# Reordering one convolution and one exponential across four engines, moving two small loads, and turning TensorE's unrolled head groups into a loop

## The reference

```python
qkv = silu(causal_depthwise_conv(qkv, conv_w))            # 4 taps along the tokens
q, k = l2_normalize(q), l2_normalize(k)                   # 16 heads of 128; v: 32 heads of 128
beta = sigmoid(beta_logit)
g = -exp(a_log) * softplus(decay_logit + dt_bias)
g = cumsum(g) inside a chunk
decay = exp(where(incl, g[:, None] - g[None, :], -inf))
a_mat = where(strict, (k * beta) @ k.T * decay, 0)
sol = triangular_solve(a_mat + I, [v * beta, k * beta * exp(g)])
attn = where(incl, q @ k.T * decay, 0)
# then, chunk after chunk: v_new = u - w @ S; o = q_dec @ S + attn @ v_new; S = S * gl + k_dec.T @ v_new
o = rmsnorm(o) * norm_w * silu(z); y_dn = o @ w_dn_out
```

## Time and profile before

| | before |
|---|---|
| median of 3 runs | 2833.82 us |
| lowest and highest | 2833.7, 2834.3 us |
| the profiled execution, its own time | 2834.3 us |
| its span, first to last instruction | 2832.6 us |
| mean granted TensorE clock | 0.996 |
| PE busy | 2775.6 us, 98% |
| PEld busy | 2072.8 us, 73% |
| DVE busy | 1252.3 us, 44% |
| ACT busy | 446.0 us, 16% |
| POOL busy | 63.7 us, 2% |
| DMA | 654.12 MB, mean 231 GB/s |

### The profile page before, as it was taken

How to read it: one execution, slowest core, us unless ns; L and a number is a source line. 1 busy time by engine, 2 the same in 40 slices (tenths; PEclk the granted TensorE clock), 3 DMA queues, 4 the chain that set the end, 5 groups by cost and what they waited for, 6 DMA issues and landing times.

```text
span 2832.6 us, 53479 instructions
## 1 busy us (share of the span) xinstructions
PE 2775.6 (98%) x22343; PEld 2072.8 (73%) x22343; DVE 1252.3 (44%) x2593; ACT 446.0 (16%) x773; POOL 63.7 (2%) x115
## 2 busy tenths in 40 slices
PE   8999999999999999999999999999999999999997
PEld 8899898898898888888899999843444444444442
DVE  6566565665664327777665652221111211112114
ACT  3121121221221111110010000131112111112110
POOL 1000000000000000000000000000000000000000
PEclk9999999999999999999999999999999999999999
DMA  7233242343344523444477556378999999999997
GB/s 218 88 122 120 90 149 91 107 142 98 102 149 107 163 90 123 130 136 137 145 210 228 178 161 226 149 293 362 422 422 422 422 422 422 422 422 422 422 422 280
DMA packets 328854, 654.12 MB, mean 231 GB/s; under 512 B 45232, under 2 KB 274736, under 8 KB 279536
## 3 DMA queue, kind: packets, MB, share of 16 engines
q1 hardware_dynamic: 328688, 651.61, 62.7%
HBM read 649.49 MB, written 2.10 MB: 230 GB/s over the span
## 4 chain that ended last, share of the span: by engine, by line
PE 88%; DMA 7%; DVE 2%; DVEq 2%; issue 1%; ACT 0%; SPq 0%; ACTq 0%
PE bank L723 14%; PE bank L675 14%; PE bank L1054 10%; PE bank L1244 9%; PE bank L975 8%; PE bank L1282 7%; DMA arena<-in_w_up_dram 7%; PE bank L1223 4%; PE bank L1109 4%; PE bank L1322 4%; PE bank L800 1%; PE bank L818 1%; PE bank L938 1%; PE bank L811 1%; PE bank L1254 1%
## 5 line engine op out<-in xcount | busy, mean ns | idle before, releaser
L675 PE MATMUL bank<-arena 128*128 128x256 f32 x2048 | 484.8, 386 | 0.0
L1244 PE MATMUL bank<-arena 128*64 128x512 f32 x2048 | 445.5, 594 | 12.3 <-DMA arena<-in_w_up_dram 12.3
L675 PEld LDWEIGHTS bank<-arena 128*128 128x128 f32 x2048 | 374.9, 190 | 52.3
L723 PEld LDWEIGHTS bank<-arena 128*128 128x128 f32 x3584 | 403.9, 192 | 4.2 <-issue 3.8
L723 PE MATMUL bank<-arena 128*128 128x128 f32 x3584 | 405.5, 275 | 0.0
L1244 PEld LDWEIGHTS bank<-arena 128*64 128x64 f32 x2048 | 144.5, 137 | 311.3 <-issue 281.5
L1054 PEld LDWEIGHTS bank<-arena 128*128 128x128 f32 x2576 | 287.8, 192 | 0.1
L1054 PE MATMUL bank<-arena 128*128 128x128 f32 x2576 | 287.8, 275 | 0.0
L975 PE MATMUL bank<-arena 128*128 128x256 f32 x1024 | 223.5, 380 | 0.0
L2356 DVE TENSOR_SCALAR arena<-bank 128x512 f32<-128x512 f32 x16 | 11.1, 691 | 465.8 <-PE bank L1244 465.8
L975 PEld LDWEIGHTS bank<-arena 128*128 128x128 f32 x1024 | 194.0, 190 | 26.7
(11 more groups left out here) (341 smaller groups left out, 2412.8 us busy)
## 6 DMA issues: line engine op xcount, KB each, us to landing
arena<-in_w_in_dram SPq DMA_DIRECT2D x72, 2048.0 KB, 8.7
arena<-in_w_up_dram SPq DMA_DIRECT2D x64, 2048.0 KB, 16.5
arena<-in_w_gate_dram SPq DMA_DIRECT2D x64, 2048.0 KB, 13.9
arena<-in_w_down_dram SPq DMA_DIRECT2D x64, 2048.0 KB, 21.1
arena<-in_w_dn_out_dram SPq DMA_DIRECT2D x16, 2048.0 KB, 8.2
arena<-in_w_glu_b_dram SPq DMA_DIRECT2D x8, 2048.0 KB, 8.2
arena<-in_w_glu_a_dram SPq DMA_DIRECT2D x8, 2048.0 KB, 8.2
arena<-in_w_mix_out_dram SPq DMA_DIRECT2D x8, 2048.0 KB, 14.3
```

The source lines that it names most:

```text
L675: last = mm(ps[bank][:, ct * T:ct * T + T], ring[:, buf, k, ct * P:ct * P + P], rhs[:, k, :], start=k == 0, stop=k == KD - 1)
L723: last = mm(regions[:, 4 * bank + place % 4], left(k), right(k), start=k == 0, stop=k == KD // 2 - 1)
L1244: last = mm(ps[bank][CAP * o:CAP * o + CAP, :], xg[:, 4 * q + k, CAP * o:CAP * o + CAP], w[:, o, k], start=False, stop=q == 3 and k == 3, ...
```

## The change

It has four parts. In the prologue, SP issues dt_bias and a_log behind the three ring slots and no longer ahead of wbd. On DVE, `conv(3)` comes ahead of `decay(1)`; on ACT, `silu(3)` comes ahead of the two exponentials of c = 1. POOL no longer waits for `conv_ready` ahead of the product of c = 1. On PE, groups 0 to 6 become a hardware loop, with the group's number in a register.

```diff
@@ SP
-            sp.dma_start(dtrow, dt_bias.partition_broadcast(P)).then_inc(bias_loaded, 16)
-            sp.dma_start(arow, a_log.partition_broadcast(P)).then_inc(bias_loaded, 16)
             sp.dma_start(wbd, in_rows(w_in[:, OFF_BD:OFF_BD + 2 * H_V])).then_inc(wbd_loaded, 16)
             for r in range(3):
                 sp.dma_start(ring[:, r], in_rows(w_in[:, group_col(r, 0):group_col(r, 0) + SC])).then_inc(slot_loaded[r], 16)
+            sp.dma_start(dtrow, dt_bias.partition_broadcast(P)).then_inc(bias_loaded, 16)
+            sp.dma_start(arow, a_log.partition_broadcast(P)).then_inc(bias_loaded, 16)
             sp.dma_start(cw[:, :, :], conv_w.rearrange("(j p) t -> p j t", p=P)).then_inc(pro_loaded, 16)
@@ POOL
                 for c in range(2):
                     pool.wait_ge(dexp_ready, 2 * gi + c + 1)
-                    if c == 1:
-                        pool.wait_ge(conv_ready, 4 * gi + 4)
                     g.tensor_tensor(Dm[:, c], Dc[:, c], upper.unsqueeze(1).to_broadcast([P, GV, P]), ALU.mult)
@@ PE
-            for g in range(GROUPS - 1):
+            with pe.Fori(0, GROUPS - 1) as g:
                 group(g, True)
                 front(g + 1)
             group(GROUPS - 1, False)
@@ ACT
                 A(Dc[:, 0], Dc[:, 0], ACT.Exp)
                 act.drain()
                 act.sem_inc(dexp_ready, 1)
+                silu(3)
+
                 act.wait_ge(arg_ready, 2 * g + 2)
                 A(Eg, ps[5][:, :].rearrange("p (a t) -> p a t", a=GV), ACT.Exp)
                 A(Dc[:, 1], Dc[:, 1], ACT.Exp)
                 act.drain()
                 act.sem_inc(dexp_ready, 1)
-                silu(3)
@@ DVE
                 decay(0)
                 join_heads(3)
+                conv(3)
                 decay(1)
-                conv(3)
```

## The result

The changed kernel takes 2869.55 us (median of 4 runs, 2868.8 to 2869.89), the kernel before on the same chip 2834.03 (4 runs, 2833.7 to 2834.3). The ratio is 1.0126, 95% interval 1.0109 to 1.0142: 35.5 us slower. The forecast was 2848.5, with 2862 as its upper end: the direction was right, and the loss is two and a half times the 14.2 us forecast.

The account below looks back on a forecast made before the run. The prediction took PE as the bound, a microsecond's delay in a group moving the end by one. It summed 2834.3 + 8.6 (reorder) + 1.2 (loads) + 4.2 (back edges) = 2848.3, said 2848.5, range 2838 to 2862.

Parts of the forecast that it names:

- The reorder, 8.6 us: DVE, ACT and POOL in the head groups: chunk 1's At comes later, PE waits at L800; 7.3 + 1.3 us.
- The chain: Join, conv(3), Silu, table load, Exps, POOL, At of chunk 1: 1.04 us later a group, 1.34 in the last.
- the row at 192.91: ACT timeline before the change: Silu's table load issued at once, 3 us ahead of its activation.
- the serial rival: ACT's table load starts only after its argument has come: reorder 14 us, total 2854; chance 0.07.
- the earlier Silu buys nothing: Transposes L776: silu(3) done at 195.16 instead of 196.51, but PE is busy until 197.58 either way; gain 0.
- POOL's removed wait is free: POOL's product of c = 1: decay(1) now follows conv(3), so the Exp wait implies the removed one; cost 0.
- The back edge, 4.2 us: PE's loop: each of six back edges asks for code not fetched ahead, 0.7 us each; ends 0 and 20.
- the L951 row: PE's one idle time with no releaser inside a run of matmuls without a wait, 1.44 us; price for edges.
- Register waits at 0: PE's loop: waits numbered from registers cost 0, worked out under queued matmuls; ends 0 and 15 us.
- The moved loads, 1.2 us: Prologue: biases land at about 29.0, DVE waits 3.1 us at L1726, PE waits 1.2 us; bounds 0 and 2.5.
- The two waits that it has: Prologue: PE waits on DVE's sums for slot 1, 0.7 us, and for slot 2, 0.5 us.
- the dear edge: PE's loop: 2 to 3.4 us at each of six back edges, 12 to 20 us, total 2860; chance 0.15.

Follow-up runs that it names:

- e5: Kernel before with only POOL's wait on conv_ready removed, DVE and ACT in their old order: 2870.21 us, 1.0133.
- e7: Kernel before with the reorder, plus two z0 fill products moved between the first products of the two chunks at solve level 0: 2832.94 us, 0.9999.
- e13: Whole changed kernel, plus two z0 fill products moved between the first products of the two chunks at solve level 0: 2856.22 us, 1.0084 to the kernel before.
- e8: Kernel before with the reorder, and a copy in place of the Silu of slot 3: 2836.54 us, 1.0011.
- e3: Kernel before with only dt_bias and a_log issued behind the ring loads: 2837.09 us, 1.0017.
- e12: The changed kernel measured again on another chip: 2871.10 us, 1.0133 to the kernel before.

## Why the prediction was right in kind and short in size

**The reorder, 8.6 us: right.** The waits at L798 grew by 7.9 us. The chain held link by link: 0.97 a group against 1.04, and 1.36 of wait in the last group against 1.34. The table load was issued ahead of its argument, as taken from the row at 192.91; the serial rival is refuted. The Trainium skill (ScalarE: Activation LUTs, What ACT_TABLE_LOAD costs) makes its 2.66 us for a switch of a load of 1.28 and a drain of 1.38. The trace agrees on the load, 1.28, and shows no drain: the next activation starts 0.01 us behind the load. That the earlier Silu buys nothing, and that POOL's removed wait is free, held as well, the latter only because the new order takes its place (e5).

**The back edge, 4.2 us: the first wrong step, a mis-sized term.** "I take 0.7 for each, half of the L951 row, 4.2 us in all" measured 9.7 in the loop alone and 13.2 with the rest of the change. The mechanism was as told: the body is fetched anew in each round (12 or 13 pieces in a group's time against 10), and the edge asks for one or two that nobody fetched ahead. What failed is the halving: the matmuls queued ahead of the edge hide the transfer itself, in the loop alone, but not the time behind its landing, so that 1.4 to 1.7 us stay idle at each edge, and the full L951 row, 1.44 us, would have been right for the idle time of the loop alone. Some 2.2 us more in six rounds are in no wait that the profile shows. Register waits at 0 were right.

**An idle microsecond is not one microsecond: the second wrong step, a missing term.** The first part of the prediction says that what delays PE by a microsecond moves the end by one. The idle 1.96 us in front of the solve's thin matmuls was followed by half the clock in six of seven groups (in five on the other chip). With one fall behind an edge that makes seven, at 1.5 us a time: 10.5 us in all, in no term and no rival. Shortening the idle time to 0.9 us (e7, e13) or 1.38 (e8) removed the falls there.

**The moved loads, 1.2 us: mis-sized.** Landing was put at 29.0 and was 31.2, since dt_bias held SP for 5.92 us and a_log was issued only then; conv_w's 5.83 in the trace before had shown it. DVE was 5.3 us late, beyond the slack in front of `glog_ready`, so PE's cumulative sum waited 2.2 us, a wait that the prediction doesn't have. The two waits that it has measured 0.73 (forecast 0.7) and 0.25 (0.5).

The nearest rival was the dear edge, 2860, and it too lacks the clock. With the measured terms (reorder, edges with what comes with them, clock, loads, small waits, and the shorter stretch behind the groups) the sum is 2834.3 + 7.9 + 15.4 + 10.5 + 3.2 + 0.8 - 2.2 = 2869.9, against 2870.05 of the profiled execution.

**Open.** Why the clock falls behind the 1.96 us in two of seven groups with the reorder alone and in five or six with the loop besides. The length of the idle time alone doesn't decide: in the prologue the clock fell behind 1.65 us (e3) and 1.96 (e12) and not behind 2.21 (the changed kernel), and at the edges behind 2.08 and not behind 2.40. Why PE needs 1.5 us after a piece of code has landed, and why the hints changed nothing. What the 2.2 us are that come with six edges and show as no wait. That a body short enough to stay would have free edges is only argued, from the GLU loop.

## What to carry to other kernels

Where PE is the bound, price an idle stretch by the clock that follows as well as by its own length, and look for independent matmuls to put into it: moving two products won 5 us on the kernel before and 14 on the changed one. A loop whose body is fetched anew in each round cost 1.4 to 1.7 us of idle time at each back edge here, and up to 2.4 (3.1 once) beside the other edits; fold rounds together or leave it unrolled. Before a wait between POOL and DVE is removed, see whether it was keeping their instructions apart.

## What was not expected of the hardware

- Half the granted clock behind an idle 1.96 us of PE in the solve, not behind 1.38 us (the copy) or 0.9 (the fills), but again where idle times of 1.43 and 1.43 to 1.55 stood 2 us apart with 0.35 between (POOL's wait): four fill products take 1.63 to 2.07 us in place of 1.13.
- PE goes on 1.4 to 1.7 us after the missing piece of code has landed, with a branch hint or without.
- Convolution steps of 0.88 us that take 1.96 and 2.41 beside POOL.
- One small DMA issue that holds SP for 5.92 us behind three of 2 MB. The trace before has it too, at 5.83, and it was overlooked.
